# Early gates as sixteen pairs of seven products, with weight sums and all input projections made ahead

## What is computed

```python
h = rms_norm(x, norm_mix_pre)
proj = h @ w_in            # split into the inputs of the four branches
o_a = gated_delta_rule(...)          # then rms_norm and a silu gate
o_b = block_sweep_attention(...)     # latent attention, scores with rope
o_c = gla_chunked(...)               # gated linear attention in chunks
o_d = block_sweep_attention(..., forget_cum)   # attention with a forget gate
for i in range(N_BRANCHES):
    gate = jax.nn.sigmoid(h @ w_gate[i] + b_gate[i])
    merged = merged + gate * (branches[i] @ w_branch_up[i])
x = x + rms_norm(merged @ w_out, norm_mix_post)
# ... MLP; then the second layer, whose modulation is silu(c) @ mod_w + mod_b
```

## Time and profile before

| what | value |
|---|---|
| runs | 2730.07 us median of 3 (2725.63 to 2732.98) |
| the profiled execution | span 2728.4 us |
| TensorE busy | 2606.0 us (96%) |
| VectorE busy | 1650.5 us (60%) |
| ScalarE busy | 1145.3 us (42%) |
| POOL busy | 162.5 us (6%) |
| DMA | 289.74 MB, mean 106 GB/s |

### The profile page before, as it was taken

How to read it: one execution, slowest core, us unless ns; L and a number is a source line. 1 busy time by engine, 2 the same in 40 slices (tenths; PEclk the granted TensorE clock), 3 DMA queues, 4 the chain that set the end, 5 groups by cost and what they waited for, 6 DMA issues and landing times. The chain is left out here.

```text
span 2728.4 us, 34994 instructions
## 1 busy us (share of the span) xinstructions
PE 2606.0 (96%) x14252; PEld 2056.3 (75%) x14252; DVE 1650.5 (60%) x2135; ACT 1145.3 (42%) x1686; POOL 162.5 (6%) x290
## 2 busy tenths in 40 slices
PE   7999999999999999989999999999999999998998
PEld 6867877666867766778888878878776788877777
DVE  4375443544344366955977767666567699843844
ACT  5472122343433445543454554444578522233131
POOL 0112110000100000100121100000000000000000
PEclk9999999999999999999999999999999999999999
DMA  4323321110323212651343488752111111113241
GB/s 159 116 89 64 56 52 55 54 44 20 112 69 105 66 39 90 217 194 70 126 159 140 147 299 307 246 212 78 68 42 54 57 60 55 53 49 144 69 170 47
DMA packets 104431, 289.74 MB, mean 106 GB/s; under 512 B 11224, under 2 KB 16120, under 8 KB 104272
## 3 DMA queue, kind: packets, MB, share of 16 engines
q1 hardware_dynamic: 80976, 208.01, 22.4%
q0 software_dynamic: 23296, 79.51, 9.1%
HBM read 225.54 MB, written 61.93 MB: 105 GB/s over the span
## 5 line engine op out<-in xcount | busy, mean ns | idle before, releaser
L281 PE MATMUL psum<-mixer_in,weights_parts 128*128 128x512 f32 x2016 | 475.8, 397 | 13.4 <-PEq L184 11.3
L281 PEld LDWEIGHTS psum<-mixer_in,weights_parts 128*128 128x128 f32 x2016 | 381.9, 190 | 108.0 <-issue 22.2
L453 PE MATMUL psum<-hidden,weights_parts 128*128 128x512 f32 x1536 | 403.6, 410 | 11.1 <-ACT early_gate L477 4.6
L453 PEld LDWEIGHTS psum<-hidden,weights_parts 128*128 128x128 f32 x1536 | 283.4, 191 | 86.6 <-issue 18.0
L248 DVE TENSOR_TENSOR weights_parts<-weights_raw,weights_parts 128x1024 fp32r<-128x1024 f32 (+2 forms) x110 | 107.5, 978 | 255.0 <-ACT weights_parts L232 254.9
L281 PE MATMUL psum<-hidden,weights_parts 128*128 128x512 f32 x1104 | 253.7, 392 | 5.5 <-PEq L878 2.8
L3427 PE MATMUL psum<-mixer_in,weights_parts 128*128 128x512 f32 x1104 | 255.5, 391 | 0.0
L3427 PE MATMUL psum<-mlp_in,weights_parts 128*128 128x512 f32 x1080 | 250.9, 392 | 1.9 <-DVE weights_parts L3279 1.7
L281 PEld LDWEIGHTS psum<-hidden,weights_parts 128*128 128x128 f32 x1104 | 207.0, 188 | 52.0 <-issue 6.9
L3427 PEld LDWEIGHTS psum<-mixer_in,weights_parts 128*128 128x128 f32 x1104 | 207.3, 188 | 45.4
L3427 PEld LDWEIGHTS psum<-mlp_in,weights_parts 128*128 128x128 f32 x1080 | 202.5, 188 | 47.5 <-DVE weights_parts L3279 3.4
(11 more groups left out here) (559 smaller groups left out, 4094.8 us busy)
## 6 DMA issues: line engine op xcount, KB each, us to landing
weights_raw<-in_w_in SPq DMA_DIRECT2D x69, 512.0 KB, 3.6
hidden_sums_scratch<-y POOLq DMA_DIRECT2D x84, 256.0 KB, 2.8
weights_raw<-in_w_gate SPq DMA_DIRECT2D x32, 512.0 KB, 3.7
gate_scratch<-early_gate SPq DMA_DIRECT2D x64, 256.0 KB, 2.1
gate<-gate_scratch POOLq DMA_DIRECT2D x32, 512.0 KB, 3.6
weights_raw<-in_w_mlp_back SPq DMA_DIRECT2D x30, 512.0 KB, 5.6
weights_raw_second<-in_w_mlp_back SPq DMA_DIRECT2D x30, 512.0 KB, 4.5
mod_weights<-in_mod_w POOLq DMA_DIRECT2D x48, 256.0 KB, 3.8
```

The lines of the kernel that those rows point to most:

```text
L281: mm = nc.tensor.matmul(c.psum[:, bank + h, 0:cols], c.parts[:, s, wp, at], moving(k, xp, h), start=(n < halves), stop=(n >= halves * (3 * ...
L453: mm = nc.tensor.matmul(c.psum[:, bank, :], c.parts[:, s, wp, at], self.hidden[:, k, xp, h * HALF:(h + 1) * HALF], start=(k == 0 and n == ...
```

## The change

`EarlyGates` makes the gates in another way. The 32 units become 16 pairs. The weights of a pair are seen as a 2x2 matrix of blocks (two units by two halves of the inner dimension, 128 columns x 4 blocks each), the hidden state as 2x2 blocks (halves of the inner dimension by halves of the tokens), and their product is made of seven block products instead of eight, with sums of blocks on either side. The seven kinds come in the order 1 and 2 in turns, 6 and 7 in turns, then 4, 5, 3. Kind 2 goes on in the bank of kind 1 of the same pair after that has been copied out, kind 7 in that of kind 6. There are 112 pieces of 4 portions, 448 portions or 1344 matmuls. For each piece SP loads a block of 128x512 (256 KB), ScalarE casts it, VectorE makes its low part, and after the matmuls ScalarE copies the bank to one of four tiles; POOL stores that to one, two or three of the pair's four quarters in DRAM, for kinds 1 and 2 plainly, for the others with an addition in DRAM. The right operand is replaced five times, after pieces 29, 31, 62, 63 and 79, by a load of 128x2048, a cast and a subtraction.

All 25 projection units are made first, in one product (`projections`), together with the whole modulation (two tiles a unit), the sums of weight blocks (`GateSums`: from unit 4 to 19 a load of two units' weights, four VectorE sums, a store two units later) and the sums of hidden blocks (`GateRights`: seven VectorE operations and two stores for every four units). The fifteen units of the three later branches are stored in DRAM and loaded by SP when their branch begins.

The shares of the stages are now: delta inputs 64, chunks 128, last step 4, turn 24; latent inputs 24 (8 ahead of the sums of squares, 8 after), its attention 60; gated linear inputs 24 (8 ahead of the turn of the values, 4 ahead of the gate product, 12 after), chunks 40 (in each block three and two ahead of the state's product and none after), turn 12; forgetting inputs 24, attention by pairs 44. `hidden` is held in two halves of the tokens, and the second is given free after the projections. In `gate_and_merge` each load waits for the last kind of its pair.

The core of the diff:

```diff
+PIECE = QUARTERS
+GATE_PAIRS = 16
+FOLLOWS = {2: 1, 7: 6}
+RELOADS = (6, 7, 4, 5, 3)
+SUM_AT = {5: 0, 6: 1, 7: 2, 3: 3}
+GATE_PARTS = {1: slice(1, 4), 2: slice(0, 1), 6: slice(1, 2), 7: slice(2, 4), 4: slice(2, 3),
+              5: slice(1, 4, 2), 3: slice(1, 2)}
...
     def pe_program(self, pe):
+        for n in range(self.pieces):
+            kind = self.kind(n)
+            for j in range(QUARTERS):
+                yield PIECE * n + j
+                if j == 0:
+                    bank = self.banks[n]
+                    pe.wait_ge(self.low, n + 1)
+                    same = [m for m in range(n) if self.banks[m] == bank]
+                    if same:
+                        pe.wait_ge(self.kept, same[-1] + 1)
+                    if kind in RELOADS:
+                        pe.wait_ge(self.right_low, RELOADS.index(kind) + 1)
+                at = slice(j * P, (j + 1) * P)
+                for k, (wp, xp) in enumerate(((0, 0), (0, 1), (1, 0))):
+                    mm = nc.tensor.matmul(c.psum[:, bank, :], self.part(n, wp)[:, at],
+                                          self.right[RIGHT_SLOT[kind]][:, j, xp, :],
+                                          start=(j == 0 and k == 0 and kind not in FOLLOWS),
...
     def act_program(self, act):
+        for n in range(-3, self.pieces):
+            yield PIECE * (n + 1)
+            if n >= 0:
+                keep(n)
+            if n + 3 < self.pieces:
+                high(n + 3)
...
+            if n in RIGHT_FREE:
+                right_high(RIGHT_FREE.index(n))
...
+    def pool_program(self, pool):
+        for n in range(self.pieces):
+            yield PIECE * (n + 1) + 1
+            pool.wait_ge(self.kept, n + 1)
+            to = gate[g][GATE_PARTS[kind]].rearrange("q p n -> p q n")
+            if kind in (1, 2):
+                pool.dma_start(to, made).then_inc(self.stored[n % 4], 16)
+            else:
+                pool.dma_start(to, made, accum_op=ALU.add).then_inc(self.stored[n % 4], 16)
...
+class GateSums:
+    def on_dve(self, v, q):
+        g, tt = q - 4, self.nc.vector.tensor_tensor
+        tt(s1, a21, a22, ALU.add).then_inc(self.made, 1)
+        tt(s3, a11, a21, ALU.subtract).then_inc(self.made, 1)
+        tt(s2, s1, a11, ALU.subtract).then_inc(self.made, 1)
+        tt(s4, a12, s2, ALU.subtract).then_inc(self.made, 1)
...
+def projections(nc, c, t, hidden, small, proj, early, mod_sums, modulated):
+        def on_sp(sp, q, j):
+            m = q - lag
+            if m in stored_units:
+                sp.wait_ge(c.act_done, a0 + m + 1)
+                sp.dma_start(t["projected"][m - SMALL_UNITS], proj[:, slot(m), :]).then_inc(
+                    row_stored[slot(m)], 16)
+            rights.on_sp(sp, q)
+            gate_sums.on_sp(sp, q)
...
+        gemm(nc, c, t["w_in"], IN_UNITS, KT,
+             lambda k, part, h: hidden[h][:, k, part, :], act_per_unit=1,
+             act_epilogue=evacuate, unroll=IN_UNITS + 1, begun=True,
+             background={"sp": on_sp, "act": on_act, "dve": on_dve, "pool": modulation.load})
...
 def delta_net_inputs(nc, c, t, proj, rows, g_tok, small, padded_rows, masks, select, early,
             def _(a):
+                    early.act(a, g0 + 12 + 8 * n)
                 nc.scalar.activation(soft[gl, :], small[gl, 0, :], ACT.Abs,
                                      bias=vec(c, "row_bias")[gl, :]).then_inc(act.step("abs"), 1)
...
                         early.act(a, g0 + 24)
...
 def gated_linear_inputs(nc, c, t, proj, small, q_in, k_in, k_tail, ends, values, early,
+                sp.dma_start(gate_up[:], t["gla_gate_up"]).then_inc(c.steps["dma"], 16)
+                load(sp)
                 sp.dma_start(restart[:], t["restart"].partition_broadcast(P)).then_inc(
                     c.steps["dma"], 16)
-                sp.dma_start(gate_up[:], t["gla_gate_up"]).then_inc(c.steps["dma"], 16)
...
+                early.pe(p, e + 8)
+                p.wait_ge(loaded[1], 16)
                 turn_values(p)
-                early.pe(p, e + 4)
+                early.pe(p, e + 12)
                 p.wait_ge(c.steps["dma"], d0 + 32)
...
-                early.pe(p, e + 32)
+                early.pe(p, e + 24)
...
 def latent_inputs(nc, c, t, latent, small, q, k, v_tok, early):
+                for n in range(3):
+                    sp.dma_start(latent[:, n, :], t["projected"][LATENT_UNITS.start + n]).then_inc(
+                        loaded[n], 16)
...
+                early.pe(p, e + 8)
+                p.wait_ge(act.sem, act.value("square"))
...
-                early.pe(p, e + 24)
+                early.pe(p, e + 16)
                 p.wait_ge(vecs.sem, vecs.value("unit"))
```

More of the change, by code:

```diff
@@ new lines, in part, with uses, take @@
+    def part(self, n, x):
+        q = (n + 2) % 4
+        return self.c.parts[:, q // 2, x, (q % 2) * HALF:(q % 2 + 1) * HALF]
+    def uses(self, n):
+        return 16 * (n // 4 + 1)
+    def take(self, portions, banks):
+        start = self.planned
+        assert portions % PIECE == 0
+        first = start // PIECE
+        for n in range(first, first + portions // PIECE):
+            before = self.follows(n)
+            self.banks.append(banks[n % len(banks)] if before is None else self.banks[before])
@@ L854, in on_dve @@
         def on_dve(v, q, j):
             modulation.on_dve(v, q)
[L856 to L863 removed]
+            rights.on_dve(v, q)
+            gate_sums.on_dve(v, q)
@@ L866, in tokens_to_channels @@
+def tokens_to_channels(nc, c, o_tok, o, early, portions, banks, ahead, gate, gain):
     with ExitStack() as ctx:
@@ L2426, in attend @@
         c.base["dma"] += 16
-        e = early.take(portions)
+        e = early.take(portions, banks)
         ends, at = [], 0
```

697 lines of the change are left out of this document (435 added, 262 removed).

## The result

The changed kernel takes 2815.3 us (median of 4 runs, 2813.97 to 2817.82) against 2728.7 us for the kernel before in the same set of runs: ratio 1.0317, 95% interval 1.0304 to 1.0331. It is slower, as forecast, but by some 87 us where the forecast said 14; the time lies outside the range. The profiled execution has a span of 2813.7 us, 85.3 above the one of before.

A forecast was written before the change was run, and what follows sets the result against it. In most stages a VectorE and ScalarE chain was taken as the bound, with gate matmuls filling gaps, so the 44.1 us removed mostly became waits; stage terms summed to +13.9, span 2742.3, median 2744.0 us, range 2706 to 2764.

The forecast's parts named there:

- The clock behind new waits: Latent inputs and gated linear inputs: more idle time lowers TensorE's granted clock, +2 us (0 to +2.8) in each.
- Attention by pairs: 68 to 44 portions: narrow half saves 8 x 1.04, wide half is a loop closing without fill; -8 us (-16.5 to -2).
- the rival in which TensorE stays the bound: Wide pairs' loops have hidden slack, pitch below 8.5 us, most terms at lower bounds; -24.1, 2706 us; chance 0.2.
- the one in which the whole product counts: Whole kernel: all 44.1 us of removed gate matmuls are saved, 2686 us; chance 0.03.
- projections, +3 with an upper end of +17: All 25 units in a row: TensorE's time only moves, the risk is DMA; +3 us (0 to +17).
- the ceiling of 323: Projections, units 6 to 19: 363 GB/s asked, 323 GB/s at DMA share 0.97 taken as the most the trace shows.
- the lag of 19 us: Projections: at 323 GB/s a unit takes 12.4 us, so 14 units lag 19 us, some 14 of it taken up.
- the DMA rival: Projections bound by DMA, lag not elastic as SP issues weights behind stores and waits; +14 to +17 more, 2759 us; chance 0.15.
- delta inputs, +8.5 (+4 to +11): Piece 7 waits for a late ScalarE copy, +4 us; inserted copies, casts and subtractions delay root and reciprocal, about +4.5.
- latent attention, +4 (-2.8 to +6): 64 to 60 portions give nothing in the wide turns' loop; 15 subtractions and two right-operand reloads load VectorE; +4 us.
- gated linear chunks, -1.6: 48 to 40 portions: one between state's product and its reading goes, 0.2 of 0.69 us a block gained; -1.6 (-5.5 to +1).
- merge, 0: Merging gates: no change, since the last accumulations were issued many pieces earlier; 0 us.

The follow-up runs named there:

- mended version: Changed kernel with right sums and modulation a unit later, reloads late and in four parts, piece 5's copy, restart row and last pieces earlier: 2759.67 us, ratio 1.0107.

## Why the prediction was right and wrong

**Which step failed.** The working priced the waits from the loops and chains that TensorE stands in, and put at nothing what the order of items on the other lists makes: SP's queue, on which a store that waits for its data stands ahead of the next weights, and VectorE's and ScalarE's lists. The clock behind new waits was held at +4 us. Seven edits that move or split items, and take no work away, bring the profiled span from 2813.7 to 2758.8 us: 54.9 of the 71.4 us by which the forecast was short. How the other 16.5 us divide was not settled.

**Right: where the count goes.** Attention by pairs came out at -8.0 as forecast. From the first to the ninth start of its scores the pairs take 38.8 us instead of 45.0, and over the next six 46.6 instead of 48.0, so most of it lies in the narrow half, as forecast. The wide pairs' scores start at 1122.85 and 1131.80, a pitch of 8.95 us with a portion and a half instead of two, what it was with the fill of before.

```profile
1122.85 1.99 PE L2627 MATMUL psum<-fox_projected 64*128 64x512 f32 x8 [1.25 <-ACT fox_projected L2537]
...
1131.80 1.99 PE L2627 MATMUL psum<-fox_projected 64*128 64x512 f32 x8 [0.83 <-ACT fox_projected L2537]
```

TensorE waits for the exponential there, as forecast. With that the rival in which TensorE stays the bound falls, and so does the one in which the whole product counts. The other mechanisms named are in the trace: the wait for the first normalised unit in the latent inputs (6.15 us, with 3.86 and 4.09 ahead of it; +9.5, forecast +6 with a bound of +10.8), the restart row (4.78 us; +13.2, forecast +9.8, bound +13.8), piece 7's wait for a copy behind the logarithm (4.44, forecast 4), subtractions behind the reciprocal (2.60). The additions in DRAM were taken at 0 with a bound of +10; they are hidden but for the two places that the run with plain stores shows, some 6 us by the medians.

**Wrong: projections, +3 with an upper end of +17; measured +23.7.** The traffic was worked out rightly: 363 GB/s by the sum, 360 to 373 in the mended version's trace. Two steps failed, and the second is what cost the time. The first is the ceiling of 323, taken for the fullest stretch of the trace. It is not: the trace of before has more at 1184 us, just behind the merge's first stretch, with TensorE never idle (columns as in the earlier trace rows):

```profile
1184.00:1195.00 11.00, 11.00 (x50) 9.05 (x49) 6.08 (x6) 3.82 (x5) 0.00 (x0) 1.00 1.02 410
```

The share of 0.97 that carried 323 carried 373 in the mended version, and bursts of the changed kernel reach 414 to 423. A busy share near 1 with TensorE unhindered said that this mix of transfers filled the engines with 323, not that no other mix gets more through. But with a higher ceiling the lag of 19 us vanishes, so this step alone made the forecast too long, not too short.
By the Trainium skill, page "DMA: Bandwidth & Descriptors", section "Specifications", the limit of HBM for one core would be about 358 GB/s; the same page, section "Bandwidth", ties that figure to both cores of a pair streaming and has a core alone at more. This kernel runs on one core, and its runs agree with the second: 373 over 39 us in the mended version, and 422 over 23 us in the changed kernel (from 235 to 258). The 435 that the first section of that page gives for the fabric isn't passed in any stretch read here.
The second step is a term put at nothing: SP's list, unit by unit, with what each wait needs. It was in the text only as half a sentence of the DMA rival ("SP issues weights behind stores and waits"). A store whose data VectorE makes at that very unit stands ahead of the next weights; so does the modulation's first step ahead of a cast. Moving these two by one unit each gave 18.1 and 7.8 us (the second as the difference of two versions, 273.3 to 265.5), and the stage is then 2.2 us shorter than before.

**Wrong: delta inputs, +8.5 (+4 to +11); measured +21.2.** The two 1 MB loads ahead of the blocks were left out of the queue's account; they cost 9.4 us. What is left without them, 71.4, is +11.8, just past the end of the range.

**Wrong: latent attention, +4 (-2.8 to +6); measured +14.4.** The subtraction of 128x2048 was priced (2.4 us, it takes 2.28) but as work in a busy loop, not as one pass that stops the mask and the maximum of two turns. Splitting it leaves +9.2 in its own run and +8.5 with all seven edits, where two runs that don't touch the stage have +11.0; that the rest is the 15 inserted subtractions and copies on the loop is argued from the transposes' waits (13.4 us against 6.6), and no run takes them out.

**Wrong in sign: gated linear chunks, -1.6; measured +5.3.** The portion that went stood in the wait for the state. The text saw that the state comes when it comes, and still counted 0.2 us of the portion's time as saved in each block. Nothing was saved: blocks that nothing else disturbs follow each other at 7.55 us with 15 gate matmuls, as they did before with 18, and 0.45 us of the wait now lies open in each. Four of the seven pitches are 8.05 to 8.74 us, 3.3 us more in all; in the longest, TensorE waits 0.88 us for a piece's subtraction and 1.00 for nothing that the profile shows. And the first nine gate matmuls, behind the wait of 6.28 us, take 3.89 us instead of 2.35. Moving one portion into the wait brought 2.8 us of the stage back.

**Wrong: merge, 0; measured +6.2.** "Issued many pieces earlier" was true of all but the last piece, whose store POOL must see off before the stage ends: the first product waits 8.63 us instead of 4.14. Dealing the pieces earlier takes 10.1 us off the merge and puts 5.2 on the pairs, so half of the gain is paid there.

**Wrong in size: the clock, +4 in all.** It was charged in two stages, at 2.76 us for a piece at the lower level, where the rows have 2.4 (twelve matmuls at 0.43 instead of 0.23). TensorE's busy time is 44 us over what the matmuls cost at the rates of before, and 20.8 of it went with the waits that the seven edits removed; in the projections alone 10.4 (274.36 to 263.93 with 1152 instructions). Not all of the rest need be the clock, since short groups of matmuls also count their own ends as busy.

What is left with the seven edits, +30, is nearer the +14 that was forecast. How much of it is lost cover no run separates: in the latent inputs 4.2 us of it are TensorE's wait for the squares of rows that now come back by DMA, and in the gated linear inputs a right operand's subtraction (2.5 us in four passes) and a piece's stand last on VectorE's list, ahead of the stage's end; no run moves those two. Four portions were moved back, in one place only. And no run makes the projections ahead with the eight products of before, so the two halves of the change are not priced apart.

## What to carry to other kernels

When work is moved, write out the list of every queue that it joins, item by item with what each wait needs, before asking for bandwidth: a store that waits for data made at that moment holds up all loads behind it, and a large early load holds up the small ones that are due. Fill in a gap is worth the gap, not its own time, so taking fill away is worth nothing where a chain closes the step, and costs where the pieces that stay arrive with more casts, copies and subtractions. And charge each new wait, in a stage that TensorE fills, with the matmuls that run at the lower clock after it. A busy share near 1 in one stretch is no ceiling for the DMA: read the fullest stretches over several lengths before taking one as the limit.

## What the hardware showed that was not expected

One core's DMA moved 373 GB/s for 39 us beside a TensorE that was never idle, and up to 423 in stretches of some us, well above the 323 of the stretch that had been read the earlier trace rows; the kernel before already moved 410 for 11 us. A wait of 5.20 us was followed by twelve matmuls at 0.43 instead of 0.23 us each; one of 1.98 us at 187.80 by a run at full rate and then, from 189.2 to 192.2, at the lower one, so the price can come a few matmuls late. Stores of pieces from POOL, most of them adding in DRAM, landed in 4.2 us for 256 KB, and in 2.7 when all were plain. POOL was out of the stage 4.5 us after it had issued the last adding store, and 3.0 us after a plain one.
